# Rotary steps of the head norms moved from GpSimd to VectorE, the doubling of keys to ScalarE, in a two-block transformer kernel

## What is computed

```python
def rms_norm(x, g):
    xf = x.astype(jnp.float32)
    y = xf * lax.rsqrt(jnp.mean(xf * xf, axis=-1, keepdims=True) + NORM_EPS)
    return (y * g.astype(jnp.float32)).astype(x.dtype)

def partial_rope(x, cos, sin):        # rotates the first 16 of each head's 64 elements
    half = ROT_DIM // 2
    ...
    x1, x2, rest = x[..., :half], x[..., half:ROT_DIM], x[..., ROT_DIM:]
    return jnp.concatenate([x1 * c - x2 * s, x2 * c + x1 * s, rest], axis=-1)

# nsa_mixer (layer 0); moba_mixer (layer 1) has one k of the same kind
q = partial_rope(rms_norm(q.reshape(B, S, N_HEADS, HEAD_DIM), q_g), cos, sin)
k_cmp = partial_rope(rms_norm(compress(kc, 0), k_g[0]), cos_c, sin_c)
ks = partial_rope(rms_norm(ks.reshape(B, S, N_KV, HEAD_DIM), k_g[1]), cos, sin)
kw = partial_rope(rms_norm(kw.reshape(B, S, N_KV, HEAD_DIM), k_g[2]), cos, sin)
```

## Time and profile before

| | before |
|---|---|
| median of 3 runs | 1329.05 us |
| lowest, highest | 1327.18, 1329.94 us |
| the profiled execution | 1329.2 us |
| its span in the profile | 1327.9 us |
| mean granted TensorE clock | 0.99 |
| TensorE, VectorE, ScalarE, GpSimd busy | 1263.0, 1040.0, 596.9, 233.4 us |

### The profile page before, as it was taken

One profiled execution on the slowest core, in us unless ns is written; L12 is line 12 of the kernel. 1 busy time (PEld: TensorE's weight loads), 2 busy tenths in 40 slices (PEclk: granted clock), 3 DMA queues, 4 the chain that ended last, 5 costly groups with the idle time before them and its releaser, 6 DMA issues.

```text
span 1327.9 us, 21963 instructions
## 1 busy us (share of the span) xinstructions
PE 1263.0 (95%) x8283; PEld 1096.5 (83%) x8283; DVE 1040.0 (78%) x2322; ACT 596.9 (45%) x1105; POOL 233.4 (18%) x180
## 2 busy tenths in 40 slices
PE   5988999988999899999999999999999999999997
PEld 5677865676597569999999999999988888888886
DVE  5587896687667878999878888899877777777776
ACT  1434693546342624566554444444443343333432
POOL 0354000360000004688940000000000000000001
PEclk9999999999999989999999999999999999999999
DMA  9877631867578327355544444454566565655553
GB/s 356 294 236 264 240 137 64 291 213 248 186 276 340 112 72 277 136 193 194 175 160 143 159 144 159 144 159 144 161 215 195 191 193 194 196 192 191 193 194 104
DMA packets 92382, 256.82 MB, mean 193 GB/s; under 512 B 9472, under 2 KB 16896, under 8 KB 91904
## 3 DMA queue, kind: packets, MB, share of 16 engines
q1 hardware_dynamic: 59728, 195.91, 44.2%
q10 hardware_dynamic: 32560, 59.66, 12.6%
HBM read 254.47 MB, written 1.06 MB: 192 GB/s over the span
## 4 chain that ended last, share of the span: by engine, by line
PE 72%; DVE 14%; POOL 5%; DMA 3%; ACT 3%; issue 3%; SPq 1%; DVEq 0%; ACTq 0%; POOLq 0%
PE bank L1729 27%; PE bank L1736 26%; PE bank L693 6%; PE bank L2016 4%; PE bank L1123 3%; DVE arena L434 2%; DVE arena L970 2%; PE bank L801 2%; DMA arena<-in_w_in 2%; POOL head_ms L824 2%; DVE u_lo L685 1%; DVE arena L1010 1%; DVE v_lo L685 1%; DMA arena<-in_ada_w 1%; SPq L303 1%
## 5 line engine op out<-in xcount | busy, mean ns | idle before, releaser
L1729 PE MATMUL bank<-h_hi,u_hi 128*128 128x256 f32 x632 | 179.8, 285 | 1.1 <-ACT arena L1854 1.1
L1729 PE MATMUL bank<-h_lo,u_hi 128*128 128x256 f32 x632 | 176.1, 279 | 0.0
L1729 PE MATMUL bank<-h_hi,u_lo 128*128 128x256 f32 x632 | 176.1, 279 | 0.0
L1729 PEld LDWEIGHTS bank<-h_hi,u_hi 128*128 128x128 f32 x632 | 118.8, 188 | 1.3 <-issue 1.3
L1729 PEld LDWEIGHTS bank<-h_hi,u_lo 128*128 128x128 f32 x632 | 119.4, 189 | 0.0
L1729 PEld LDWEIGHTS bank<-h_lo,u_hi 128*128 128x128 f32 x632 | 119.4, 189 | 0.0
L2112 ACT ACTIVATE u_hi<-raw 128x1024 fp32r<-128x1024 f32 x64 | 68.0, 1062 | 104.3 <-PE bank L1736 104.3
L2112 ACT ACTIVATE v_hi<-raw 128x1024 fp32r<-128x1024 f32 x64 | 68.0, 1062 | 101.1 <-PE bank L1736 101.1
L2173 POOL TENSOR_SCALAR raw<-raw 128x1024 f32<-128x1024 f32 x1 | 2.8, 2812 | 624.4 <-DMA raw<-in_final_g 624.4
L1729 PE MATMUL bank<-h_hi,v_hi 128*128 128x256 f32 x392 | 110.9, 283 | 0.0
L434 DVE CUSTOM_DVE_ANT_0 arena<-arena 128x1024 f32<-128x1024 f32 x80 | 102.6, 1295 | 8.6 <-DMA arena<-in_ada_t 7.4
(11 more groups left out here) (277 smaller groups left out, 3431.1 us busy)
## 6 DMA issues: line engine op xcount, KB each, us to landing
raw<-in_u SPq DMA_DIRECT2D x128, 512.0 KB, 3.4
raw<-in_v SPq DMA_DIRECT2D x128, 512.0 KB, 3.6
arena<-in_ada_t SPq DMA_DIRECT2D x80, 512.0 KB, 5.0
arena<-in_ada_w SPq DMA_DIRECT2D x12, 512.0 KB, 12.2
raw<-in_nsa_w_in ACTq DMA_DIRECT2D x3, 2048.0 KB, 11.9
arena<-in_moba_w_in ACTq DMA_DIRECT2D x3, 2048.0 KB, 13.6
arena<-in_w_in ACTq DMA_DIRECT2D x3, 2048.0 KB, 10.4
arena<-in_w_query ACTq DMA_DIRECT2D x3, 2048.0 KB, 10.4
```

Source lines behind the costliest of these rows:

```text
L1729: last = pe.matmul(zbank[k].t[:, 0:S], u[:, c, :], h[:, c, :], start=n == 0, stop=n == 3 * DC - 1)
```

## The change

The four rotary steps are issued on VectorE, directly behind its own two multiplies, with a wait for the second multiply before the first step and a wait for the third step before the fourth. The doubling of the keys becomes an activation (Copy) on ScalarE that waits for the fourth step. GpSimd keeps the powers, and the copy for the compressed keys (L1361).

```diff
@@ -833,14 +833,14 @@
-        G.need(m, m_rope)
+        V.need(m, m_rope)
...
-        G.did(po.tensor_tensor(t3[:, :, ROT:ROT + HALF], d3[:, :, HALF:ROT], s_lo, ALU.mult))
-        G.did(po.tensor_tensor(t3[:, :, ROT + HALF:2 * ROT], d3[:, :, 0:HALF], s_hi, ALU.mult))
-        m = G.did(po.tensor_tensor(t3[:, :, 0:ROT], d3[:, :, 0:ROT], cc, ALU.mult))
-        G.need(m)
-        return m_src, G.did(po.tensor_tensor(d3[:, :, 0:ROT], t3[:, :, 0:ROT], t3[:, :, ROT:2 * ROT], ALU.add))
+        V.did(ve.tensor_tensor(t3[:, :, ROT:ROT + HALF], d3[:, :, HALF:ROT], s_lo, ALU.mult))
+        V.did(ve.tensor_tensor(t3[:, :, ROT + HALF:2 * ROT], d3[:, :, 0:HALF], s_hi, ALU.mult))
+        m = V.did(ve.tensor_tensor(t3[:, :, 0:ROT], d3[:, :, 0:ROT], cc, ALU.mult))
+        V.need(m)
+        return m_src, V.did(ve.tensor_tensor(d3[:, :, 0:ROT], t3[:, :, 0:ROT], t3[:, :, ROT:2 * ROT], ALU.add))
@@ -889,10 +889,10 @@
-                G.need(mk)
-                mk = G.did(po.tensor_copy(dup.rearrange("p (g u d) -> p g u d", g=NKV, u=2),
-                                          kn[:, 0:NKV * HD].rearrange("p (g d) -> p g d", g=NKV).unsqueeze(2).broadcast_to(
-                                              [P, NKV, 2, HD])))
+                A.need(mk)
+                mk = A.did(ac.activation(dup.rearrange("p (g u d) -> p g u d", g=NKV, u=2),
+                                         kn[:, 0:NKV * HD].rearrange("p (g d) -> p g d", g=NKV).unsqueeze(2).broadcast_to(
+                                             [P, NKV, 2, HD]), ACT.Copy))
```

## The result

The changed kernel took 1339.47 us in the median of ten runs, the kernel before 1330.36 in ten beside them; the ratio is 1.0064 with a 95% interval of 1.0046 to 1.0081. In a second comparison it was 1.0075, interval 1.0053 to 1.0096 (1341.95 us). The change makes the kernel slower by 8.5 to 10 us; the forecast was 10.2 us and 1339.

What follows compares the result with a forecast made beforehand. Head norms were taken as paced by a ring across ScalarE, VectorE, GpSimd and TensorE, with the doubling's wait holding ScalarE's in-order queue. 4.1 + 4.9 + 1.2 = 10.2 us gave 1339 us, range 1331 to 1349.

Steps and rivals of the forecast that it cites:

- Stretch A: Layer 0's first key tile to the second (50 to 85 us): v_hi pair and square wait behind the doubling; +4.1 us.
- Stretch B: Second key tile to the attention (85 to 158 us): ScalarE's L1315 waits behind the doubling, delaying TensorE's fold; +4.9 us.
- the whole 3.95: In stretch B, the fold's (L1333) delay behind L1315, handed on in full through z0's load; +3.95 us.
- The last 0.95 of B: Second query tile's steps stand ahead of the gate additions (L1404), which ScalarE and then TensorE wait for; +0.95 us.
- Stretch C: Layer 1's projections (248 to 310 us): A over again, but the L869 wait and low-clock time come back; +1.2 us.
- Rival 1: In stretch B, q1's load takes its 11.9 us and binds, costing 3 to 6 us more: 1345 us; 17%.
- Rival 2: Holds partly covered, with cheaper rotary steps and faster powers: half of A and B, 1334 us; 12%.
- Rival 3: Shorter ring, holds where ScalarE had nothing due; waits for L893 and L843 (2.5 and 2.7 us) go: 1324 us; 7%.
- Rival 4: The change does nothing, as each hold ends inside a wait that another load sets: 1329 us; 5%.

Runs made afterwards that it cites:

- tile 0's hold alone: Against the kernel with the doubling later: tile 0's doubling put back where the change has it, tile 1's left later; 1341.02 us, ratio 1.0094.
- the holds of tile 0 and tile 1: Against the kernel with the doubling later: only tile 0's doubling put back, ratio 1.0094, or only tile 1's, ratio 1.0074.

## Why the prediction was right, and where it was not

**The sum.** Forecast 1339 us, +10.2; measured +8.5 and +10.0. That the 1339.47 us of the first comparison meet the 1339 so closely is in part luck, as the kernel before took 1330.36 us there and not the 1329.05 that the forecast started from. In the trace, net: A + B to the first L970 +9.2 (forecast 9.0), C +1.35 from layer 1's first L820 (1.2).

**Stretch A: right, step by step.** Steps of a key tile on VectorE 55.73 to 56.41, 0.7 us (0.75); of a query tile 0.9 us (0.9); doubling 0.63 (0.6). With 0.56 us taken off, the v_hi pair ran at 56.4 (56.4), the square of the second tile at 58.3 (58.4), u_lo at 71.6 (71.6), TensorE's first product with it at 72.8 (72.9). kv1's load was issued at 64.1 (64.1). That the kernel with the doubling later in the same queue is at 1.0000 shows the cause, not only the size.

**Stretch B: size right, carrier wrong.** L1315 ran at 105.34; 4.1 for A and 0.56 on top of the forecast's 100.7 make 105.36. TensorE stood 2.85 us for it. The step that failed is the next: "z0's load ... its parts feed the next projection, so the whole 3.95 goes through". TensorE in fact made good part of the delay, as its old wait of 2.48 us for GpSimd's doubled key was gone: by the last matmul of q1's tile 1 it was only 5.3 us late net, not 8. What carries the delay begins in the chain of the changed kernel, in order of time (start, us, what):

```profile
104.55 0.23 DVE arena L843
104.84 0.50 issue
105.34 0.36 ACT hkT L1315
105.70 0.95 ACT u_hi L682
...
111.57 6.95 PE bank L693 x30
118.56 2.17 DVE arena L1298 x7
120.73 0.60 DVE head_ms L820
```

The chain puts 6.95 us of TensorE ahead of L1298, but VectorE's timeline shows no wait there. Before:

```profile
98.05 2.42 DVE L685 TENSOR_TENSOR u_lo<-raw,u_hi 128x1024 fp32r<-128x1024 f32 x2
...
109.17 2.50 DVE L1298 TENSOR_TENSOR arena<-arena 128x120 f32<-128x120 f32 x8
```

After:

```profile
106.68 2.36 DVE L685 TENSOR_TENSOR u_lo<-raw,u_hi 128x1024 fp32r<-128x1024 f32 x2 [1.91 <-ACT u_hi L682]
...
118.24 2.49 DVE L1298 TENSOR_TENSOR arena<-arena 128x120 f32<-128x120 f32 x8
...
126.45 2.35 DVE L685 TENSOR_TENSOR u_lo<-arena,u_hi 128x1024 fp32r<-128x1024 f32 x2
```

q1's high parts stand behind L1315, so VectorE's low parts of q1 come at 106.68 (98.05 before) after a wait of 1.91 us, and from there VectorE works almost without a gap up to its additions L1298 at 118.24 (109.17 before) and the square's sum L820 at 120.65 (111.92). TensorE's matmuls and ScalarE's square that this sum needs were done at 117.8. So on VectorE 8.2 us net are found that TensorE no longer has. z0's high parts ran only at 125.13, after 7.36 us of waiting for the load, and this looks like the cause; but VectorE got to their low parts at 126.45, when the first was ready at 126.2. The load was late by as much as VectorE was. That it could be taken out of the way with nothing gained that shows, in either kernel, shows that VectorE's queue carried the delay. That B's size came out is in part luck: the path over z0's load was later by as much as the one that counted. I had followed one resource through the stretch and stopped at the first that gave the right number.

**The last 0.95 of B** was +0.5 (between the multiply L831 of q1's tile 0 and the gates L1404: 14.43 us before, 14.92 after): two sets of steps, 1.8 us, less a wait of 0.97 for u_hi that had covered one of them, and less 0.3 as the first pair of low parts is shorter (2.63 us before, 2.35 after).

**Stretch C: right.** The u_lo pair of 278.72 is at 292.98, which is 4.6 us later (4.6) once the 9.67 us are taken off by which the layer's first L820 is later. The wait before L869 is gone, the granted clock stays at 1.00 from 300 to 312, TensorE's first scores of layer 1 (L959) are at 317.77 against 308.03, 9.7 later, so C itself is 0 there, as forecast, and VectorE, behind with its products, adds 1.3. (Those products waited for their own loads 2.46 us before L970 in the kernel before and 2.59 after, so the loads' waits made hardly a difference.) The kernel with the steps moved for layer 1's last query tile alone shows the gain that the change buried: 2.9 us net.

**Rival 1** (the loads bind, 17%) did not come: q1's load was used at 105.60, 9.0 us after its issue, without a wait, as it took 7.9 us, not 11.9. It was near: with tile 0's hold alone this very load bound. **Rival 2** (holds partly covered) would have been 1334; the path that sets the time got no such cover. **Rival 3** (faster) had its mechanism right in one place only, which is worth 2.9 us alone. **Rival 4** is what the steps without the doubling's move do.

**A wrong premise without effect.** I read the 4.15 us of the earlier trace rows as GpSimd's speed, and said that the trace agreed on it with the Trainium skill's Perfetto Trace Analysis, section Optimizing GPSIMD Operations, which calls GpSimd generally slower. With VectorE idle the steps take 1.15 us against VectorE's 0.7: GpSimd is the slower one, but by 0.45 us and not by 3.4. The rest of the 4.15 us was the price of running beside VectorE's low parts and its product L434. The trace of the kernel before had a sign of it in the next tile, where the way from L839 (62.03) to the copy (64.20) took 2.17 us. The forecast didn't rest on it, as it took the steps' end from VectorE alone, but the expectation for the doubling alone did, and missed by it.

## What to carry to other kernels

Before an operation moves to another in-order queue, write down what stands behind the wait it brings, and put it where its input is already there: the same doubling on the same engine cost 10 us ahead of the v_hi pair and nothing that the timing shows (within 2 us) behind it. Move only the instance whose wait nothing covers: one query tile's four steps gained 2.9 us, all fifteen norms' gained nothing. And where two paths end about a microsecond apart, taking one away shows little of either: the holds of tile 0 and tile 1, 7.0 and 8.8 us net at the first L970 when alone, made 9.2 together.

## What the runs showed of the hardware

GpSimd's duration for one and the same step depends on what VectorE does beside it: L839 on 128x32 elements took 0.26 us with VectorE idle (the kernel with the doubling alone moved) and 1.17 beside its subtraction of two SBUF tiles; the 128x512 copy 0.61 and, in the kernel with the steps alone moved, 1.54. VectorE pays as well: the pair of low parts took 2.36 us alone and 2.76 beside GpSimd's copy. The Trainium skill, SBUF — State Buffer, section Who interferes with whom, says that a VectorE instruction with two inputs in SBUF contends with a GpSimd instruction that reads SBUF. The trace agrees: 1.17 us is about the length of one of the two low parts (2.41 / 2), as if the step had waited for its end. That section says of VectorE's two-port modes that who issues first has the shared pair for the whole instruction; for a subtraction of two SBUF tiles it doesn't say so, and the 1.17 us look like it.
